# Attention values in column halves, with the output born transposed and the head norm made by a product with ones

## The chip, the cores and the metric

The kernel runs on one core of a Trainium2 chip. The metric is the device time of one execution in microseconds. The engines are named as in the profile: PE (TensorE, with PEld for its weight loads), DVE (VectorE), ACT (ScalarE), POOL (GpSimd) and SP (SyncE, which only issues DMAs here). Each runs its own instructions in order and waits on semaphores; POOL also issues DMAs.

## The reference, cut to what matters

One residual block over 1024 tokens of width 1024: RMS norm, one projection, stick-breaking attention (8 heads of 64) beside gated linear attention (GLA, 4 heads), an output projection, then a routed mixture of 32 experts. The part that the change touches:

```python
for i in range(T // Q_BLOCK):                       # 8 query tiles of 128, keys up to kend
    z = einsum('bqhd,bshd->bhqs', qb, kb) * scale
    a = where(strict, exp(log_sigmoid(z) + tail), 0.0)
    outs.append(einsum('bhqs,bshd->bqhd', a, vb))   # the value product
sb = rms_norm(sb, sb_out_norm_g)                    # per head: mean over its 64 columns
h = h + concat([sb, go], axis=-1) @ w_out
```

All inputs are float32. The output projection and the experts split each operand in a high and a low part and make three products of them (`three`).

## The kernel before, in words

**Stages.** First the projections (to about 249 us). Then attention: 48 steps, one for each query tile i (0 to 7), pair of heads (0 to 3) and up to 512 keys, so a tile of i < 4 has four steps of width 128(i+1), a later one has four of 512 and four of the rest. Then the W_out stage: one output tile after another, eight in all, with the GLA state recurrence, the norm and the routing of the tile before woven in. Last the experts, in blocks of 128 rows.

**An attention step** n, as the engines' loops have it (PE's loop at line 958, ACT's at 1379, DVE's at 1720): PE makes the scores of both heads (`scores`, line 876, each head in its 64 rows of the array), ACT evicts them twice with a sigmoid (1388, 1391), DVE scans them (1731) and multiplies (1736), PE turns the result two steps later (`turn_a`, 893), ACT copies it out (`prob`, 1399), and PE multiplies it with the values three steps later (`values`, 912). There the turned probabilities are the weights (128 keys x 128 queries) and 64 value columns of one head stream through; the output has queries on its partitions and all eight heads side by side in one bank. When a tile is complete, ACT squares it into `o_sq` (1363) and copies it to `o_sb` (1364), and DVE sums the squares by head (1724).

Between scores and transposes and again before the values, PE has `fill` products: 12 units of 8 k steps that make the GLA queries and the output gate. Their place is planned by `fill_plan`, over the first 40 steps, by the width of the steps. Unit f from the fifth on waits until DVE has taken the gate of the unit before it out of bank 7 (`gate_ready`, line 1743).

**The norm and the projection.** The eight-column means of tiles 0 to 6 go through Ln and Exp at once on ACT (1411, 1412), the last tile's after the stage. POOL multiplies tile by tile (`norm_sb`, 618). PE then turns the tile (`turn_sb`, 990), ACT and DVE split it in its high and low part (`sb_high` 1428, `sb_low` 1603), and the W_out products take it as weights.

**Order in the W_out stage.** The orders are written out by hand. PE's loop at 1033 has eight k steps of six products a tile; `read_states`, `turn_h`, `keys_values(t + 2, 0)` (line 934, which waits for `gv_in` from DRAM), `route`, `turn_sb`, `keys_values(t + 2, 1)` and `turn_gla` stand behind named k steps. ACT's loop at 1467, iteration w: `square_h(w-1)`, `go_square(w+1)`, `rstd_h`, `evict_h`, `go_rstd`, `sb_high`, `go_high`, `route_exp(w-1)`. `square_h(t)` writes `v_row[t % 2]` and from t = 2 on waits until the rows of tile t-2 have been scattered (`own_scattered`, line 1440). DVE's loop is at 1876. POOL's loop at 655, for t = 1 to 7: `load_gv(t + 1)`, `load_gate(t)`, `norm_sb(t + 1)`, and from t = 3 on `scatter_own(t - 3)` and `scatter_given(t - 3)`, two indirect DMAs each; ahead of it stand `load_gv(0)`, `load_gv(1)`, `load_gate(0)`, `norm_sb(0)`, `norm_sb(1)`. `norm_sb` waits for one of two counts only:

```python
pool.wait_ge(sb_rstd, 1 if t < TILES - 1 else 2)
```

## Time and profile before

| what | value |
|---|---|
| median of 3 runs | 1219.95 us (1219.72 to 1222.05) |
| profiled execution | 1218.32 us, span 1216.6 us |
| mean granted PE clock | 0.990 |
| busy: PE, DVE, ACT, POOL | 1170.6, 857.5, 732.0, 295.1 us |
| value products (line 912), 576 passes | 69.6 us busy, mean 270 ns |
| weight loads of these | 70.5 us, mean 191 ns |
| scans on DVE (line 1731), 96 | 94.0 us, mean 1020 ns |

All times inside the execution are counted from the start of the span. A float32 product shows as two passes, each a weight load and a matmul. Of passes merged into one row the given time runs from the first start to the last end, and the ends of matmuls are modelled, so a row reaches some 0.2 us into what follows; start-to-start distances are the safer reading. Line numbers of the form L765 are those of the kernel below; L765 to L767 are the three products of `three`, whoever calls it.

### The profile page before, as it was taken

The page shows a single profiled execution, that of the slowest core. Times are in us where ns is not written, and L with a number is a line of the kernel's source. Part 1 is how long each engine was busy: PE and PEld are TensorE (multiplying, and loading weights), DVE is VectorE, ACT ScalarE, POOL GpSimd, SP SyncE. Part 2 cuts the span into 40 slices and gives each one's busy share as a digit, 9 for nine tenths or more (in the row PEclk, how much of TensorE's full clock was granted, in tenths as well). Part 3 has the DMA queues.
Part 4 walks back from the last instruction along what each step waited for, and adds up shares of the span by engine and source line. Part 5 has one row for each costly group of instructions (what it writes and reads, how often), then busy time and mean ns, then how long its engine had stood idle before and what let it go on. Part 6 is the DMA issues. An engine that isn't in the chain of part 4 may idle for free. (4 is left out here: it accounts for less than half of the span.)

```text
span 1216.6 us, 17187 instructions
## 1 busy us (share of the span) xinstructions
PE 1170.6 (96%) x6164; PEld 959.6 (79%) x6164; DVE 857.5 (70%) x975; ACT 732.0 (60%) x894; POOL 295.1 (24%) x250
## 2 busy tenths in 40 slices
PE   5999999999989998999989999999999999999997
PEld 4897777877867776777877878888888888888886
DVE  6721212267656689677677999888988988988894
ACT  5532222366535585232356887887888788788873
POOL 3300000010000002132243236343433433222322
PEclk9999999999989999999989999999999999999999
DMA  8155443010000033356688999999999999999992
GB/s 267 45 188 210 141 162 113 1 53 19 26 18 18 19 122 113 114 190 242 252 298 311 331 385 403 379 400 382 376 384 399 378 380 394 386 367 386 393 377 56
DMA packets 71029, 288.18 MB, mean 237 GB/s; under 512 B 16224, under 2 KB 23409, under 8 KB 46402
## 3 DMA queue, kind: packets, MB, share of 16 engines
q1 hardware_dynamic: 51538, 238.30, 50.8%
q0 software_dynamic: 14064, 30.31, 9.0%
q10 hardware_dynamic: 5376, 18.88, 3.9%
q8 instruction: 33, 0.54, 0.2%
q14 instruction: 18, 0.15, 0.0%
HBM read 248.82 MB, written 54.80 MB: 250 GB/s over the span
## 5 line engine op out<-in xcount | busy, mean ns | idle before, releaser
L1603 DVE TENSOR_TENSOR ew_l<-raw,ew_h 128x2048 fp32r<-128x2048 f32 x192 | 430.7, 2284 | 0.0
L1422 ACT ACTIVATE ew_h<-raw 128x2048 fp32r<-128x2048 f32 x192 | 364.9, 1921 | 53.2 <-PE banks L767 46.4
L765 PE MATMUL banks<-ew_h,xb_h 128*128 128x512 f32 x520 | 205.8, 396 | 1.9 <-issue 1.6
L767 PE MATMUL banks<-ew_h,xb_l 128*128 128x512 f32 x520 | 202.9, 390 | 0.0
L766 PE MATMUL banks<-ew_l,xb_h 128*128 128x512 f32 x520 | 202.5, 389 | 0.0
L1731 DVE TENSOR_TENSOR_SCAN tails<-tails 128x512 f32<-128x512 f32 (+3 forms) x96 | 94.0, 1020 | 62.5 <-ACT tails L1388 62.5
L765 PE MATMUL banks<-win_h,u_h 128*128 128x512 f32 (+1 forms) x320 | 122.6, 383 | 2.8 <-DVE u_l L1603 2.5
L766 PE MATMUL banks<-win_l,u_h 128*128 128x512 f32 (+1 forms) x320 | 118.9, 372 | 0.0
L767 PE MATMUL banks<-win_h,u_l 128*128 128x512 f32 (+1 forms) x320 | 118.8, 371 | 0.0
L765 PEld LDWEIGHTS banks<-ew_h,xb_h 128*128 128x128 f32 x520 | 98.0, 188 | 21.9 <-issue 1.9
L767 PEld LDWEIGHTS banks<-ew_h,xb_l 128*128 128x128 f32 x520 | 97.6, 188 | 20.9
L766 PEld LDWEIGHTS banks<-ew_l,xb_h 128*128 128x128 f32 x520 | 97.7, 188 | 19.2
L765 PE MATMUL banks<-ew_h,a_h 128*128 128x512 f32 x248 | 99.3, 401 | 0.0
L767 PE MATMUL banks<-ew_h,a_l 128*128 128x512 f32 x248 | 97.0, 391 | 0.0
L766 PE MATMUL banks<-ew_l,a_h 128*128 128x512 f32 x248 | 96.8, 390 | 0.0
L702 POOL DMA_INDIRECT out_dram<-y_row,scatter_row x31 | 51.3, 1654 | 158.7 <-ACT y_row L1517 146.5
L601 POOL TENSOR_TENSOR z_l<-z_raw,z_h 128x1024 fp32r<-128x1024 f32 x6 | 14.6, 2437 | 303.2 <-ACT z_h L1308 303.2
L1388 ACT ACTIVATE tails<-banks 128x1024 f32<-128x1024 f32 (+3 forms) x48 | 39.4, 821 | 70.0 <-PE banks L880 58.6
L694 POOL DMA_INDIRECT xb<-rows_dram,gather_idx x28 | 74.4, 2659 | 22.7 <-POOL gather_idx L691 21.6
L912 PEld LDWEIGHTS banks<-v_s,prob 128*128 128x128 f32 x576 | 70.5, 191 | 3.2 <-issue 0.4
L765 PEld LDWEIGHTS banks<-win_h,u_h 128*128 128x128 f32 x320 | 60.5, 189 | 15.6 <-issue 6.1
L912 PE MATMUL banks<-v_s,prob 128*128 128x64 f32 x576 | 69.6, 270 | 0.0
(248 smaller groups left out, 1991.2 us busy)
## 6 DMA issues: line engine op xcount, KB each, us to landing
raw<-in_expert_w_gate SPq DMA_DIRECT2D x64, 1024.0 KB, 8.6
raw<-in_expert_w_down SPq DMA_DIRECT2D x64, 1024.0 KB, 7.2
raw<-in_expert_w_up SPq DMA_DIRECT2D x64, 1024.0 KB, 7.6
rows_dram<-zero_rows ACTq DMA_DIRECT2D x8, 2048.0 KB, 7.6
win_raw<-in_w_in SPq DMA_DIRECT2D x16, 512.0 KB, 5.1
x_in<-in_x SPq DMA_DIRECT2D x8, 512.0 KB, 9.4
raw<-in_w_out SPq DMA_DIRECT2D x4, 1024.0 KB, 4.8
h_row<-in_x SPq DMA_DIRECT2D x8, 512.0 KB, 6.2
```

The costliest lines, as they stand in the source:

```text
L601: nc.gpsimd.tensor_tensor(z_l[b % 2][:, :, :], z_raw[b % 2][:, :, :], z_h[b % 2][:, :, :].bitcast(fp32), SUB).then_inc(z_l_ready, 1)
L694: pool.indirect_dma_start(out=xb[:, :], out_offset=None, in_=rows_dram, in_offset=bass.IndirectOffsetOnAxis(ap=gather_idx[:, :], axis=0), ...
L702: pool.indirect_dma_start(out=out_rows, out_offset=bass.IndirectOffsetOnAxis(ap=row[:, 0:1], axis=0), in_=y[:, :], in_offset=None, bounds_ ...
L765: mm(ps, lh, rh, start=start, stop=False)
L766: mm(ps, lh, rl, start=False, stop=False)
L767: return mm(ps, ll, rh, start=False, stop=stop)
L912: last = mm(o_bank[:, SB_DIM * hd:SB_DIM * (hd + 1)], prob[n % 2][:, h, P * j:P * j + P], v_s[:, u["lo"] // P + j, SB_DIM * hd:SB_DIM * (h ...
L1388: A(tails[u["row"] % 2][:, :, u["col"]:u["col"] + u["w"]], z, ACT.Sigmoid, scale=-1.0).then_inc(c_done, 1)
L1422: A(ew_h[slot % SPLIT][:, :], raw[raw_slot][:, :], ACT.Copy).then_inc(ew_h_ready, 1)
L1603: return V.tensor_tensor(dst, src, high.bitcast(fp32), SUB)
L1731: last = V.tensor_tensor_scan(out=part, data0=part, data1=part, initial=1.0 if u["top"] else row[:, h, c1:c1 + 1], op0=MUL, op1=ALU.min)
```

## The change

In `values` the operands are swapped. The value columns of one head (128 keys x 64) are the weights, the turned probabilities (128 keys x 128 queries) stream through, and head h of the pair writes partitions 64h to 64h+63 of the bank: the output has head dimensions on its partitions and queries along the columns, that is, it is born transposed. The two heads of a pair alternate. `turn_sb` is gone.

The sum of squares by head now runs across partitions: `mean_o` multiplies the squared tile with `head_ones`, two 64x64 blocks of ones, in one product of 512 columns, which gives every element its head's mean. ACT makes the factor of a whole tile by Ln and Exp over 128x512 (`rstd_o`) into `o_rs`, which holds one tile, and POOL multiplies two full tiles. DVE's reductions over `o_sq` are gone. `square_o` reads the copied tile, no longer the bank. `sb_high` and `sb_low` read `o_t` in place of bank 4. Tile 0 gets split buffers of its own, so that it is split while attention still ends.

The order around it: `mean_o(0)` and `mean_o(1)` stand in PE's steps 48 and 50, `mean_o(t + 2)` behind k = 6 of W_out tile t. W_out(0) now begins without waiting for `turn_gla(0)` and `keys_values(1, 0)`, which stand behind its k = 1 and k = 0. On ACT `rstd_o(w + 1)` and `square_o(w + 2)` stand at the head of iteration w, and on DVE `sb_low(0)` ahead of `go_mean(0)`. POOL's loop keeps its order; `norm_sb(t)` waits for the factor of its own tile. `turn_h` waits for `sb_rstd` where it waited for `sb_mixl`. SP loads `gain2` after the first mean and not after the last.

```diff
...
@@ -178,10 +177,14 @@
         gate_out = at("gate_out", R3 + 66 * KB, [P, HALF])
-        o_sb = at("o_sb", R1 + 96 * KB, [P, TILES, HALF])
+        o_t = at("o_t", R1 + 96 * KB, [P, TILES, HALF])
+        o_sq = at("o_sq", R1 + 70 * KB, [P, HALF])
+        mix_first_h = at("mix_first_h", R1 + 72 * KB, [P, PAIRS, P], f32r)
+        mix_first_l = at("mix_first_l", R1 + 74 * KB, [P, PAIRS, P], f32r)
 
...
         wo_l = at("wo_l", R1 + 32 * KB, [P, KT, D], f32r)
+        o_rs = at("o_rs", R1 + 64 * KB, [P, HALF])
         gv_in = [at("gv_in0", R3 + 42 * KB, [P, HALF]), at("gv_in1", R1 + 66 * KB, [P, HALF])]
...
@@ -613,10 +617,8 @@
             def norm_sb(t):
-                pool.wait_ge(sb_rstd, 1 if t < TILES - 1 else 2)
-                rows = o_sb[:, t, :].rearrange("p (h n) -> p h n", n=SB_DIM)
-                nc.gpsimd.tensor_tensor(rows, rows, o_rs[:, t, :].rearrange("p (h a) -> p h a", a=1).broadcast_to(
-                    [P, SB_HEADS, SB_DIM]), MUL).then_inc(sb_normed, 1)
+                pool.wait_ge(sb_rstd, t + 1)
+                nc.gpsimd.tensor_tensor(o_t[:, t, :], o_t[:, t, :], o_rs[:, :], MUL).then_inc(sb_normed, 1)
 
...
@@ -906,13 +908,24 @@
                         pe.wait_ge(kq_out, 2 * TILES)
-                for h in range(2):
-                    hd = 2 * u["pair"] + h
-                    for j in range(u["w"] // P):
-                        last = mm(o_bank[:, SB_DIM * hd:SB_DIM * (hd + 1)], prob[n % 2][:, h, P * j:P * j + P],
-                                  v_s[:, u["lo"] // P + j, SB_DIM * hd:SB_DIM * (hd + 1)], start=first and h == 0 and j == 0,
-                                  stop=True, skip_group_check=True)
+                for j in range(u["w"] // P):
+                    for h in range(2):
+                        hd = 2 * u["pair"] + h
+                        last = mm(o_bank[SB_DIM * h:SB_DIM * (h + 1), P * u["pair"]:P * (u["pair"] + 1)],
+                                  v_s[:, u["lo"] // P + j, SB_DIM * hd:SB_DIM * (hd + 1)], prob[n % 2][:, h, P * j:P * j + P],
+                                  start=first and j == 0, stop=True, skip_group_check=True)
                 last.then_inc(pv_done, 1)
+
+            def mean_o(t):
+                pe.wait_ge(o_squared, t + 1)
+                if t < 2:
+                    pe.wait_ge(beta_done, NZ - 1 + t)
+                else:
+                    pe.wait_ge(sb_rstd, t)
+                    if t >= 3:
+                        pe.wait_ge(vt_ready, t - 2)
+                mm(bank[2 * t if t < 2 else 4], head_ones[:, :], (o_sq if t else o_sq_first)[:, :], start=True,
+                   stop=True).then_inc(o_mean, 1)
 
...
@@ -961,6 +974,10 @@
                 fill(n, 0)
+                if n == NZ:
+                    mean_o(0)
+                if n == NZ + 2:
+                    mean_o(1)
                 if 2 <= n < NZ + 2:
...
@@ -1027,9 +1034,6 @@
 
-            turn_sb(0)
-            turn_gla(0)
-            keys_values(1, 0)
             for t in range(TILES):
...
@@ -1041,28 +1045,31 @@
                         col = slice(HALF * half, HALF * half + HALF)
-                        last = three(bank[2 * (t % 2) + half], mix_h[t % 2][:, k, :], mix_l[t % 2][:, k, :],
+                        mh, ml = (mix_first_h, mix_first_l) if t == 0 and k < 4 else (mix_h[t % 2], mix_l[t % 2])
+                        last = three(bank[2 * (t % 2) + half], mh[:, k, :], ml[:, k, :],
                                      wo_h[:, k, col], wo_l[:, k, col], start=k == 0, stop=k == KT - 1)
...
                         rank_tile(t - 2)
+                    if t == 0 and k in (0, 2):
+                        keys_values(1, k // 2)
                     if t == 0 and k == 1:
-                        keys_values(1, 1)
-                    if k == (0 if t else 2) and t + 1 < TILES:
+                        turn_gla(0)
+                    if k == (0 if t else 4) and t + 1 < TILES:
                         read_states(t + 1)
...
                         turn_h(t - 1)
-                    if k == (2 if t else 3) and t + 2 < TILES:
+                    if k == (2 if t else 5) and t + 2 < TILES:
                         keys_values(t + 2, 0)
...
                         route(t - 1)
-                    if k == 3 and t + 1 < TILES:
-                        turn_sb(t + 1)
-                    if k == 4 and t + 2 < TILES:
+                    if k == (4 if t else 6) and t + 2 < TILES:
                         keys_values(t + 2, 1)
-                    if k == 5 and t + 1 < TILES:
+                    if k == (5 if t else 7) and t + 1 < TILES:
                         turn_gla(t + 1)
+                    if k == 6 and t + 2 < TILES:
+                        mean_o(t + 2)
                     if k == 5 and t == TILES - 1:
...
@@ -1357,11 +1364,22 @@
                 act.wait_ge(pv_done, m + 1)
-                if i:
-                    act.wait_ge(o_mean, i)
                 o_bank = bank[7 if i == TILES - 1 else 6]
-                A(o_sq[:, :], o_bank, ACT.Square, scale=SB_DIM ** -0.5).then_inc(o_squared, 1)
-                A(o_sb[:, i, :], o_bank, ACT.Copy).then_inc(o_out, 1)
+                A(o_t[:, i, :], o_bank, ACT.Copy).then_inc(o_out, 1)
+
+            def square_o(t):
+                act.wait_ge(o_out, t + 1)
+                if t == 1:
+                    act.wait_ge(qk_done, NZ)
+                if t >= 2:
+                    act.wait_ge(o_mean, t)
+                A((o_sq if t else o_sq_first)[:, :], o_t[:, t, :], ACT.Square, scale=SB_DIM ** -0.5).then_inc(o_squared, 1)
+
+            def rstd_o(t):
+                act.wait_ge(o_mean, t + 1)
+                if t:
+                    act.wait_ge(sb_normed, t)
+                rstd_of(o_rs[:, :], bank[2 * t if t < 2 else 4], eps_col[:, :]).then_inc(sb_rstd, 1)
 
...
@@ -1374,6 +1392,15 @@
                 rstd_of(go_rs[:, :], go_ms[:, :], eps_col[:, :]).then_inc(g_rs, 1)
+
+            def sb_high(t):
+                act.wait_ge(sb_normed, t + 1)
+                if t == 1:
+                    act.wait_ge(pv_done, NZ)
+                if t >= 2:
+                    act.wait_ge(wo_done, t - 1)
+                A((mix_h[t % 2][:, 0:4, :] if t else mix_first_h[:, :, :]), o_t[:, t, :].rearrange("p (k n) -> p k n", n=P),
+                  ACT.Copy).then_inc(sb_mixh, 1)
 
...
@@ -1405,12 +1432,14 @@
                     wo_high(WO_SPLIT[n])
+                if n == FILL_SLOTS // 2:
+                    square_o(0)
                 if n == NZ:
                     nc.scalar.preload_act_table_set("natural_log_exp_and_others")
-                    act.wait_ge(o_mean, TILES - 1)
-                    link(A(o_rs[:, 0:TILES - 1, :], o_ms[:, 0:TILES - 1, :], ACT.Ln, bias=eps_col[:, :]))
-                    A(o_rs[:, 0:TILES - 1, :], o_rs[:, 0:TILES - 1, :], ACT.Exp, scale=-0.5).then_inc(sb_rstd, 1)
+                    rstd_o(0)
+                    square_o(1)
                 if n == NZ + 1:
+                    sb_high(0)
                     go_square(0)
...
@@ -1459,13 +1482,14 @@
 
-            sb_high(0)
             evict_o(TILES - 1, NZ - 1)
             go_high(0)
-            act.wait_ge(o_mean, TILES)
-            rstd_of(o_rs[:, TILES - 1, :], o_ms[:, TILES - 1, :], eps_col[:, :]).then_inc(sb_rstd, 1)
             for w in range(TILES):
                 t = w + 1
+                if t < TILES:
+                    rstd_o(t)
+                if w + 2 < TILES:
+                    square_o(w + 2)
                 if w:
...
@@ -1763,7 +1783,8 @@
                 dve.wait_ge(sb_mixh, t + 1)
-                low(mix_l[t % 2][:, 0:4, :], bank[4].rearrange("p (k n) -> p k n", n=P), mix_h[t % 2][:, 0:4, :]).then_inc(sb_mixl, 1)
+                mh, ml = (mix_h[t % 2][:, 0:4, :], mix_l[t % 2][:, 0:4, :]) if t else (mix_first_h[:, :, :], mix_first_l[:, :, :])
+                low(ml, o_t[:, t, :].rearrange("p (k n) -> p k n", n=P), mh).then_inc(sb_mixl, 1)
 
...
@@ -1863,16 +1884,14 @@
             wo_low(2)
+            sb_low(0)
             go_mean(0)
             go_norm(0)
-            sb_low(0)
             next_state(2)
...
             wo_low(3)
-            dve.wait_ge(o_squared, TILES)
-            V.reduce_sum(o_ms[:, TILES - 1, :], heads(o_sq[:, :]), axis=AX.X).then_inc(o_mean, 1)
             for w in range(TILES):
...
```

## Rows read from the trace of the kernel before

**Rows 1.** Busy time by stage: engines' busy us (instructions), PE clock, DMA share, GB/s

```profile
248.70:433.40 184.70, 178.89 (x1129) 140.27 (x1128) 119.98 (x138) 103.06 (x153) 13.85 (x9) 0.98 0.08 25
433.40:476.30 42.90, 40.30 (x315) 32.12 (x314) 40.00 (x41) 36.25 (x42) 4.25 (x6) 1.00 0.43 153
...
534.87:589.00 54.13, 52.71 (x322) 41.26 (x321) 41.00 (x139) 15.41 (x42) 17.98 (x20) 1.00 0.64 238
...
607.00:650.00 43.00, 38.10 (x204) 32.37 (x203) 33.03 (x85) 24.28 (x31) 15.23 (x14) 0.88 0.78 271
...
650.00:1216.00 566.00, 556.93 (x2628) 466.28 (x2628) 489.54 (x323) 441.86 (x372) 202.50 (x145) 1.00 0.96 365
```

**Rows 2.** Timeline of PE around value products: start, us, what, count

```profile
399.99 0.40 PE L767 MATMUL banks<-u_h,z_l 128*128 128x512 f32 x1
400.23 1.89 PE L912 MATMUL banks<-v_s,prob 128*128 128x64 f32 x16
...
406.21 1.00 PE L912 MATMUL banks<-v_s,prob 128*128 128x64 f32 x8
```

**Rows 3.** Timeline of PE: a full-array product, and column-half products of the GLA group

```profile
108.77 0.60 PE L832 MATMUL banks<-log_g,suffix 128*128 128x256 f32 x2
109.20 0.50 PE L834 MATMUL banks<-chunk_sel,log_g 128*128 128x2 f32 x4
...
537.05 1.09 PE L947 MATMUL banks<-state,gq_t 128*64 128x256 f32 x8
...
541.61 0.40 PE L767 MATMUL banks<-wo_h,mix_l 128*128 128x512 f32 x1
541.93 0.66 PE L934 MATMUL banks<-gv_in,k_dec 64*64 64x128 f32 x8
```

**Rows 4.** What fill products waited for (us, times); busy time after the longest wait

```profile
  DVE gate_out L1743: 5.8, 3
...
356.50:360.00 3.50, 3.46 (x9) 2.78 (x10) 1.88 (x3) 0.00 (x0) 0.00 (x0) 0.52 0.22 80
```

**Rows 5.** Timeline at the turn to W_out, in brackets idle before; busy time after it

```profile
472.76 2.48 DVE L1694 SCALAR_TENSOR_TENSOR wo_l<-raw,mix_gain,wo_h 128x1024 fp32r<-128x1024 f32 x2
...
478.63 0.50 PE L765 MATMUL banks<-wo_h,mix_h 128*128 128x512 f32 x1
...
485.04 1.09 PE L947 MATMUL banks<-state,gq_t 128*64 128x256 f32 x8 [1.23 <-DVE state L1711]
...
492.52 0.70 PE L934 MATMUL banks<-gv_in,k_dec 64*64 64x128 f32 x8 [2.21 <-DVE state L1711]
...
493.10:496.50 3.40, 3.40 (x13) 2.67 (x11) 1.47 (x5) 0.00 (x0) 0.00 (x0) 0.51 0.02 5
```

**Rows 6.** Timeline of POOL, ACT and DVE during one W_out tile (w=3)

```profile
534.09 1.05 POOL L618 TENSOR_TENSOR o_sb<-o_sb,o_rs 128x512 f32<-128x512 f32 x1
541.02 1.04 POOL L642 DMA_INDIRECT rows_dram<-v_row,dest  x1 [5.88 <-DVE dest L1857]
...
545.96 0.59 POOL L607 DMA_DIRECT2D gv_in<-gv_dram  x1
...
536.16 0.20 ACT L1460 ACTIVATE stat<-stat 128x1 f32<-128x1 f32 x1 [2.21 <-DVE stat L1821]
539.35 1.06 ACT L1441 ACTIVATE v_row<-h_row 128x1024 f32<-128x1024 f32 x1 [2.98 <-DVE h_row L1785]
...
542.20 1.06 ACT L1452 ACTIVATE v_t<-banks 128x512 f32<-128x512 f32 x2
...
540.08 0.15 DVE L1857 SCALAR_TENSOR_TENSOR dest<-rank,expert_of 128x2 int32<-128x2 f32 x1
```

**Rows 7.** Timeline of PE in that tile: the transposes that leave

```profile
545.72 0.63 PE L990 MATMUL banks<-ident,o_sb 128*128 128x128 f32 x4
```

**Rows 8.** Landing of gv loads, from issue; the wait for a landed scatter

```profile
DMA to landing us min/median/max: 3.0/3.5/6.6
...
POOL xb L667 <- DMA rows_dram<-v_row,dest: 6.3, 1, 6.3
```

More of the change, by code:

```diff
@@ L110, in hybrid_block_kernel @@
         kq_rs = const("kq_rs", [P, 2, SB_HEADS])
-        o_ms = const("o_ms", [P, TILES, SB_HEADS])
-        o_rs = const("o_rs", [P, TILES, SB_HEADS])
+        head_ones = const("head_ones", [P, P])
         glr_s = const("glr_s", [P, 2, RANK])
@@ L453, in _ @@
                 sp_e.dma_start(h_row[n][:, :], x_t[n]).then_inc(hx[n], 16)
-            sp_e.wait_ge(o_mean, TILES)
+            sp_e.wait_ge(o_mean, 1)
             sp_e.dma_start(gain2[:, :], ffn_norm_g.partition_broadcast(P)).then_inc(gain2_in, 16)
@@ L547, in link @@
                 pool.wait_ge(psmall, chain[0])
-            for tile, value in ((ident, 0.0), (causal_neg, 0.0), (suffix, 0.0), (chunk_sel, 0.0), (before, 1.0),
+            for tile, value in ((ident, 0.0), (causal_neg, 0.0), (suffix, 0.0), (chunk_sel, 0.0), (head_ones, 0.0), (before, 1.0),
                                 (ones_b, 1.0), (eps_col, EPS)):
@@ L555, in _ @@
                 nc.gpsimd.memset(suffix[r, r], 1.0 / TAU)
+                nc.gpsimd.memset(head_ones[r, r], 1.0)
                 last = nc.gpsimd.memset(chunk_sel[r, b:b + 1], 1.0 / TAU)
@@ L981, in turn_gla @@
                 last.then_inc(g_turned, 1)
-            def turn_sb(t):
-                pe.wait_ge(sb_normed, t + 1)
-                if t:
-                    pe.wait_ge(sb_mixl, t)
-                if t >= 2:
-                    pe.wait_ge(vt_ready, t - 1)
-                for p in range(PAIRS):
-                    last = nc.tensor.transpose(bank[4][:, P * p:P * p + P], o_sb[:, t, P * p:P * p + P], ident[:, :])
-                last.then_inc(sb_turned, 1)
             def turn_h(t):
                 pe.wait_ge(h_ready, t + 1)
-                pe.wait_ge(sb_mixl, min(t + 2, TILES))
+                pe.wait_ge(sb_rstd, min(t + 3, TILES))
                 pe.wait_ge(g_mixed, min(t + 2, TILES))
@@ L1422, in high @@
                 A(ew_h[slot % SPLIT][:, :], raw[raw_slot][:, :], ACT.Copy).then_inc(ew_h_ready, 1)
-            def sb_high(t):
-                act.wait_ge(sb_turned, t + 1)
-                if t >= 2:
-                    act.wait_ge(wo_done, t - 1)
-                A(mix_h[t % 2][:, 0:4, :], bank[4].rearrange("p (k n) -> p k n", n=P), ACT.Copy).then_inc(sb_mixh, 1)
             def go_high(t):
@@ L1436, in square_h @@
                 if t == 1:
-                    act.wait_ge(sb_turned, 2)
+                    act.wait_ge(sb_mixl, 2)
                 if t >= 2:
@@ L1720, in _ @@
             for n in range(NZ + 4):
-                if n - 4 in TILE_END and n - 4 < NZ - 1:
-                    i = TILE_END[n - 4]
-                    dve.wait_ge(o_squared, i + 1)
-                    V.reduce_sum(o_ms[:, i, :], heads(o_sq[:, :]), axis=AX.X).then_inc(o_mean, 1)
                 if n < NZ:
```

6 lines of the change are left out of this document (3 added, 3 removed).

## The prediction

> **What bounds the kernel now.** I read the stages first. From 248.7 to 433.4 us (attention, while the fill products still run) PE is busy for 178.89 of 184.70 us and DVE for 119.98: PE paces it. From 433.4 to 476.3 (last query tile, no fill left) DVE is busy for 40.00 of 42.90 us, PE 40.30, ACT 36.25: the scans and their wait for ACT share the pace. The W_out stage, three tiles of it from 534.87 on, has PE at 52.71 of 54.13 us, so PE paces that too, 18.0 us a tile, but the chain of norm, routing and gate beside it is nearly as long. The 566 us of experts that follow are PE at full clock; whatever the earlier stages gain or lose is handed on whole [rows 1]. The profiled execution took 1218.3 us (span 1216.6), 1.6 below the median 1219.95, so sums carry over as they are.
>
> **The products themselves.** An old value product of a 512-wide step issues 16 passes and takes 1.89 us, a 256-wide one 8 passes in 1.00: 0.445 us for each 128 keys of a head pair [rows 2]. The new form issues as many passes, each with 64 weight columns and 128 moving ones, the two heads in different column halves. The trace has this shape in the state products of the GLA group: 8 passes of 128 columns in 0.65 us, though a 256-column pass on the full array starts 0.22 us before the next (two in 0.43), that is 0.11 for 128 columns: 8 in a row would be 0.88 plus their latency. Two must run at once. The state reads say it for 128 rows: 8 passes of 256 columns in 1.09 us, against 8 x 0.22 = 1.7 one after another [rows 3]. So 0.65 us for 256 keys and, 4 more passes being 2 x 0.11, 0.87 for 384, 1.09 for 512, 0.43 for 128; old, by 0.445 for each 128 keys up or down from the two rows, 1.00, 1.45, 1.89 and 0.56. Entering halves costs: from the last fill pass to a column-half product 0.32 us, to an old value product 0.24 [rows 2, 3]; 0.09 is lost per step. Leaving is the same, as the old one also had to switch, to the scores' row halves. Net per step 0.71, 0.49, 0.26 and 0.04 us for widths 512, 384, 256, 128. Up to the end of the fill there are 16, 8, 8 and 8 such steps: 11.4 + 3.9 + 2.1 + 0.3 = 17.7 us. (Upper end, if the first pair's longer gap falls under the switch: 20.)
> The Trainium skill (TensorE: Matmul & The Clock Gate, Part 3, The mechanism) says that a weight load overlaps a running matmul only where the row group differs; both heads here use all 128 rows, so by it the load of every pair would stand bare. By it, with the page's load time (64 columns over 1.2, 53 ns, an estimate from that page), each pair would cost 0.05 us more and the 17.7 us that come next would be 6. The trace disagrees: the state reads are such halves with all 128 rows, and 4 pairs x 0.22 us of streaming plus the 0.2 tail already fill their 1.09 us [rows 3].
>
> **What of it reaches the end.** The fill must wait for DVE's gate product after each fill unit: three waits, 5.8 us in all, today [rows 4]. The gate hangs on the scan of the same step, not on PE, so what the value product between saves there is lost: about 1.4 us over seven units. After the longest of them PE ran 3.5 us at clock 0.52, the lower of its two levels (1.2 GHz) [rows 4]; if one more wait grows long enough for that it costs up to 1.7 us. In the last tile's 8 steps PE would save 5.7 us, but DVE and ACT are as full as PE: only the removed reduction and Square (0.7 us) count. Attention: -17.0 us.
> The turn to W_out: now PE waits for states (1.23 and 2.21 us) and then runs 3.4 us at clock 0.51 [rows 5]. After the change sb_low(0) comes ahead of go_mean on DVE, behind wo_low(2), which ends at 475.2; so W_out(0) can start at 476.0 and not at 478.6 [rows 5], and the states are made under its first products. Against this stand the mean product before values(47) (two passes of 512 columns, 0.86 us by twice the 256-column row [rows 3]) and the Ln and Exp over 128x512 on ACT (1.2 us by the 1.06 of two 128x512 copies plus their link [rows 6]), before prob(47). I take -5 us (-2.6 if all waits are only moved, -6.5 if all vanish). Each later tile: turn_sb leaves (four transposes, 0.63 us with a tail of 0.2 that the next products cover [rows 7]), mean_o comes with 0.86 and a switch: +0.5, six times, 3 us; norms on POOL stay 1.05.
>
> **The queue that is easy to miss.** o_rs now holds one tile, and rstd_o(w+1) is made at the head of ACT's iteration w, behind route_exp(w-2). Before, norm_sb(t+1) in POOL's loop found its factor ready: at 534.09, ahead of W_out(3), it normed tile 5 [rows 6]. Now POOL stands there until iteration w = t begins. Queued behind it, in order, are scatter_own(t-3), scatter_given(t-3), load_gv(t+2), load_gate(t+1). Take w=3. route_exp ends at 536.36, Ln and Exp end at 537.6, the norm at 538.75. Four scatters follow; today they take from their release by dest (540.23) to the gv load at 545.96: 5.7 us [rows 6]. The gv load is issued at 544.5 and lands 3.5 us later by the median of such loads (3.0 to 6.6) [rows 8]: 548.0. PE wants this tile at 541.93 [rows 3]: a wait of 6.1 us (5.6 to 9.2) where there is none, since today the load runs a tile ahead. In parallel square_h(2), which overwrites v_row, waits for scatter_own(0), issued by 541.9 and landed at 545 to 547.7 (3.0 after issue by the quickest such load; 6.3 is the one wait for this scatter that shows [rows 8]), instead of 539.35; its chain up to the copied transposes takes 3.9 us (539.35 to 543.26 today [rows 6]) and so ends at 548.9 to 551.6, where PE then stands before the logits. Less 0.4 for turn_sb, 5.7 to 7.2 us per tile for w = 3, 4 and 5. PE's idle of that length was followed by half clock in both places that rows 4 and 5 show; 3.4 us of it cost 1.7. I take 8 us x 3 = 24. In w=6 there is no gv load, but square_h(5) and so route(5) wait the same way: 7.5 us. For w = 0 to 2 no scatter is in the way and the gv load is late by 0.3 to 1.6 us: 2.5 in all. w=7 has no norm. Sum of this stage: +34 us, bounds 20 (no half clock, w=6 absorbed, waits at their low ends) and 42.
>
> **Sum.** -17.0 - 5 + 3 + 34 = +15; the slack before the experts, where PE is busy 38.10 of 43.00 us [rows 1], may take back 3 to 4 of it. Forecast +11.5 us: 1231.5. Ends: -20 - 6.5 + 3 + 20 = -3.5, and -14 - 2.6 + 3 + 42 = +28.
>
> **Rivals.**
> A. The POOL wait costs little: POOL's loop finds the factor early enough, or loads and scatters still come ahead of need. For: POOL is busy 17.98 of 54.13 us [rows 1], and its queue stands 5.88 us at a time for nothing [rows 6]. Against: order, not load, is what holds it. Then -17 - 5 + 3 + 3 = -16, 1204 us: faster. It decides if the gv row lands by the third k of each W_out tile.
> B. Column halves don't run together in this accumulating form, or their loads stand bare. Then 128 keys cost 4 x 0.109 = 0.44 us as before, the switches 40 x 0.09 = 3.6 us come on top, and attention goes from -17 to +4: 1252 us, or about 1241 if only half is lost. For: the only such rows are short bursts of 8. Against: those rows [rows 3].
> C. The stall is there but partly hidden (scatter issue shorter without DVE beside it, landing at 3 us, no half clock): +20 for the stage, time 1215 to 1224, about no change.
>
> **How the numbers follow.** Forecast (stall whole, 1224 to 1242) 0.62; A 0.15; C 0.13; B 0.10. The likeliest one's own range is 1224 to 1242. The range for 8 in 10 takes in C and part of A and of B: 1207 to 1243. Measured differences under 0.2% (2.4 us) can't be told from none. Slower by more: the forecast and B, 0.72. Same: half of C, 0.07. Faster: A and the other half of C, whose low end has the longest attention gain, 0.21.
>
> **What would show it.** Value products of a 512-wide step in about 1.1 us and 16 passes; stage up to the end of fill about 168 us long instead of 184.7; gate waits in all 7 to 8 us; W_out(0) starting 2.6 us earlier after the last value product. In W_out: state products (L934) waiting for DMA gv_in by 6 us in three tiles; POOL's norm at the head of each tile and scatters behind it; square_h waiting for rows_dram; tiles 3 to 6 of 24 to 26 us; clock near 0.9 there. Wrong would be: a value step above 1.5 us (B), W_out tiles of 18 to 19 us throughout (A), or a last attention tile that becomes shorter by over 3 us, which would mean DVE did not pace it.

## The result and the profile after

| | before | changed |
|---|---|---|
| median | 1219.84 us (1217.78 to 1222.05, 10 runs) | 1226.33 us (1223.26 to 1235.67, 10 runs) |
| ratio | | 1.0066, interval 1.0044 to 1.0088 |
| profiled execution | 1218.32 us, span 1216.6 | 1223.26 us, span 1221.5 |
| mean granted clock | 0.990 | 0.986 |

Slower by 6.5 us. The forecast was 1231.5 with 1224 to 1242 as its own range. The kernel before was timed again beside each group of experiments, with medians of 1220.1 to 1221.3 us, and the ratios given below are to those; times of different groups can differ by some 1.5 us for that alone. The two profiled executions lie 4.9 us apart; their balance is drawn up below, and it leaves out what the median has beyond it. The ten executions of the changed kernel spread over 12.4 us, those of before over 4.3, and the slowest (1235.67) has a mean clock of 0.972, the fastest 0.986: the slower an execution, the lower its clock.

The page of the changed kernel: PE is busy for 12.6 us less than before (1170.6), in a span that is 4.9 us longer.

```profile
span 1221.5 us, 17171 instructions
...
PE 1158.0 (95%) x6148; PEld 923.7 (76%) x6148; DVE 849.9 (70%) x967; ACT 741.2 (61%) x906; POOL 290.5 (24%) x253
```

Its timeline of PE around value steps (start, us, what, passes) answers to [rows 2, 3]: 1.09 us for 512 keys and 0.88 for 384, where the old form took 1.89 and some 1.45. The first value pass starts 0.32 us after the last fill pass.

```profile
403.19 0.40 PE L769 MATMUL banks<-u_h,z_l 128*128 128x512 f32 x1
403.51 0.88 PE L914 MATMUL banks<-prob,v_s 128*64 128x128 f32 x12
...
408.25 1.09 PE L914 MATMUL banks<-prob,v_s 128*64 128x128 f32 x16
```

Its stages answer to [rows 1] (columns as there; then one row for each of the W_out tiles 2 to 6). The last fill product starts at 417.14 us where it stood at 431.32. In the W_out tiles look at PE's busy time against the length: tile 2 is full, in each of tiles 3 to 6 PE is idle for 3.2 to 5.3 us, and in tiles 3 to 5 its busy time has itself grown, from 17.89 to between 19.53 and 19.93 us, for the same products: that is the clock of 0.86 to 0.93.

```profile
248.70:417.90 169.20, 163.10 (x1122) 110.44 (x1122) 116.27 (x130) 101.27 (x148) 12.55 (x6) 0.98 0.09 27
417.90:460.50 42.60, 35.35 (x328) 22.52 (x323) 40.84 (x43) 37.35 (x42) 4.29 (x7) 1.00 0.45 161
...
496.87:514.76 17.89, 17.89 (x104) 13.66 (x103) 13.42 (x45) 6.79 (x18) 2.56 (x3) 1.00 0.48 158
514.76:540.02 25.26, 19.93 (x105) 15.16 (x104) 13.40 (x45) 6.75 (x18) 6.71 (x7) 0.86 0.55 175
540.02:563.94 23.92, 19.53 (x106) 14.87 (x105) 13.43 (x45) 6.79 (x18) 6.67 (x7) 0.93 0.54 195
563.94:587.52 23.58, 19.64 (x108) 15.01 (x107) 13.42 (x45) 6.67 (x17) 6.67 (x7) 0.93 0.49 178
587.52:609.69 22.17, 18.96 (x90) 15.28 (x89) 8.89 (x33) 5.64 (x16) 11.09 (x10) 0.85 0.62 227
```

What PE waited for from 456 us to 640 (us in total, times, longest): the load that was in time before (in tile 3 the product that takes it follows at once [rows 3]) now is late, in tiles 3, 4 and 5 (5.3, 4.4 and 3.9 us, and 0.8 in tile 1); in tile 6, which has no such load, the router waits for ACT.

```profile
PE banks L947 <- DMA gv_in<-gv_dram: 14.4, 4, 5.3
PE banks L1017 <- ACT v_t L1475: 3.2, 1, 3.2
```

And why, in POOL's timeline of tile 3 (idle before in brackets). It answers to [rows 6]: there the norm ran at 534.09, ahead of W_out(3); here POOL stands 15.3 us for ACT's factor, and the four scatters, which had been free to go, and the load of the GLA rows come behind it. ACT's two rows below show the second arm of the stall: the row buffer `v_row` is free again only when the scatter has landed, and `route` waits for `v_t`, which ACT copies behind that write in its own queue.

```profile
515.36 1.28 POOL L621 TENSOR_TENSOR o_t<-o_t,o_rs 128x512 f32<-128x512 f32 x1 [15.32 <-ACT o_rs L1208]
516.82 1.08 POOL L644 DMA_INDIRECT rows_dram<-v_row,dest  x1 [0.17 <-DVE given L1860]
518.20 1.01 POOL L644 DMA_INDIRECT rows_dram<-v_row,dest  x1 [0.30 <-issue]
519.51 0.98 POOL L652 DMA_INDIRECT table_dram<-given,dest  x1 [0.30 <-issue]
520.80 0.98 POOL L652 DMA_INDIRECT table_dram<-given,dest  x1 [0.30 <-issue]
521.78 0.60 POOL L611 DMA_DIRECT2D gv_in<-gv_dram  x1
```

```profile
515.18 0.61 ACT L1376 ACTIVATE o_sq<-o_t 128x512 f32<-128x512 f32 x1
525.01 1.06 ACT L1464 ACTIVATE v_row<-h_row 128x1024 f32<-128x1024 f32 x1 [9.21 <-DMA rows_dram<-v_row,dest]
```

Two windows show what the wait leaves behind: PE idle for 5.3 us, and then 3.4 us of full work at clock 0.50. The record of the clock has it at this level for 6.8 us, from 524.1 to 530.9, so it fell while PE stood, and 4.3 us of it lie on work.

```profile
521.30:526.60 5.30, 0.01 (x2) 0.01 (x2) 0.00 (x0) 1.59 (x3) 1.86 (x3) 0.76 0.61 102
526.60:530.00 3.40, 3.40 (x14) 2.59 (x15) 1.38 (x4) 2.32 (x8) 0.00 (x0) 0.50 0.01 2
```

Starts in the two profiled executions, us, read from the trace:

| start of | before | changed | difference |
|---|---|---|---|
| last fill product | 431.32 | 417.14 | -14.2 |
| last value pass | 475.62 | 460.28 | -15.3 |
| W_out(1) | 499.36 | 478.10 | -21.3 |
| W_out(3) | 534.87 | 514.76 | -20.1 |
| W_out(7) | 604.99 | 609.69 | +4.7 |
| first expert product | 636.51 | 640.37 | +3.9 |
| end of the span | 1216.6 | 1221.5 | +4.9 |

Tiles 3 to 6 took 18.07, 18.09, 18.09 and 15.86 us before, and 25.26, 23.92, 23.57 and 22.17 after: +24.8 us, against the 20.1 won ahead of them.

### The profile page after: what moved, and what is told of

The parts are those of the page before. It is cut to its first block and busy times, and to the rows that moved or that the text cites. A ratio compares the mean times of both kernels' runs of the same rounds, so it can differ in the third digit from the quotient of the medians.

```text
span 1221.5 us, 17171 instructions
## 1 busy us (share of the span) xinstructions
PE 1158.0 (95%) x6148; PEld 923.7 (76%) x6148; DVE 849.9 (70%) x967; ACT 741.2 (61%) x906; POOL 290.5 (24%) x253
## 5 line engine op out<-in xcount | busy, mean ns | idle before, releaser
L605 POOL TENSOR_TENSOR z_l<-z_raw,z_h 128x1024 fp32r<-128x1024 f32 x6 | 14.6, 2440 | 294.4 <-ACT z_h L1315 294.4
L769 PEld LDWEIGHTS banks<-win_h,u_l 128*128 128x128 f32 x320 | 60.4, 189 | 10.6
L768 PEld LDWEIGHTS banks<-win_l,u_h 128*128 128x128 f32 x320 | 60.6, 189 | 9.2
```

Of the source, the lines that this page charges most:

```text
L605: nc.gpsimd.tensor_tensor(z_l[b % 2][:, :, :], z_raw[b % 2][:, :, :], z_h[b % 2][:, :, :].bitcast(fp32), SUB).then_inc(z_l_ready, 1)
L768: mm(ps, lh, rl, start=False, stop=False)
L769: return mm(ps, ll, rh, start=False, stop=stop)
```

## Experiments on the stall

### The norm in its turn

The changed kernel with one edit in POOL's loop: tile t is normed in iteration t and not one iteration ahead. Its factor is made in ACT's iteration t-1, so it is there when POOL comes.

```diff
-            norm_sb(1)
...
-                if t + 1 < TILES:
-                    norm_sb(t + 1)
+                norm_sb(t)
```

> The changed kernel with one thing moved in POOL's loop: norm_sb(t) stands in loop step t in place of norm_sb(t+1), so POOL waits for the factor of tile t only after load_gv(t+1), load_gate(t) and the scatters of the step before have been issued. Theory 1 (the whole loss is POOL's in-order queue standing at norm_sb): W_out tiles 3 to 6, now 25.3, 23.9, 23.6, 22.2 us, go back to 18.1, 18.1, 18.1, 15.9 plus about 0.5 each for the mean product, no PE wait for gv_in, no ACT wait for rows_dram; time 1226.3 - 23 = 1203 (1198 to 1208), ratio to before 0.982 to 0.990. Theory 2 (the Ln and Exp over whole tiles on ACT and the mean products stretch the chain of each W_out tile, POOL only shows it): tiles stay above 21 us, time above 1215.

Measured: 1198.18 us (5 runs), ratio 0.9818 (0.9804 to 0.9832). The W_out tiles from 1 on take 17.95, 17.89, 17.93, 17.93, 17.99 and 15.52 (tile 6, 15.86 before); the waits for the GLA rows and for the scattered rows are gone. POOL's timeline of this kernel: the norm now waits 2.29 us for its factor, and the scatters wait for their own data (`dest`), not for the norm; the load is issued at 505.47 and used at 519.86.

```profile
496.14 1.28 POOL L621 TENSOR_TENSOR o_t<-o_t,o_rs 128x512 f32<-128x512 f32 x1 [2.29 <-ACT o_rs L1206]
500.53 1.08 POOL L643 DMA_INDIRECT rows_dram<-v_row,dest  x1 [3.10 <-DVE dest L1876]
...
505.47 0.61 POOL L611 DMA_DIRECT2D gv_in<-gv_dram  x1
```

So the whole loss of the change, and some 21 us that it had won, hung on one position in one queue. The second theory is out, since the Ln and Exp over whole tiles and the mean products are all still there. This version is faster than both kernels.

### The same wait put into the kernel before

The kernel before with a wait of the same kind ahead of the norm, for a signal that ACT gives at about the time at which the changed kernel's factor comes.

```diff
                 if t + 1 < TILES:
+                    if t >= 2:
+                        pool.wait_ge(r_ratio, t - 1)
                     norm_sb(t + 1)
```

> The kernel before with one wait added: in POOL's loop norm_sb(t+1) waits, from t=2 on, for r_ratio >= t-1, which ACT signals at the end of route_exp(t-2), the point behind which the changed kernel makes the factor. Nothing else is changed. Theory 1: PE waits for gv_in in W_out tiles 3 to 5 and for the routing chain in tile 6, as in the changed kernel, about 1.3 us less per tile since no Ln and Exp stand between; tiles 3 to 6 longer by 4 to 6 us each, time 1219.8 + 19 = 1239 (1234 to 1246). Theory 2: POOL's waiting has cover, time 1220 to 1225.

Measured: 1249.81 us (4 runs), ratio 1.0236 (1.0211 to 1.0261). The mechanism is confirmed, for the new attention and the ones product are not in this kernel: PE waits for the GLA rows in tiles 3, 4 and 5. The size is a miss, some 10 us above what I had expected. Tiles 3 to 6 take 29.51, 23.12, 28.09 and 22.07 us, although the waits (below) are no longer than in the changed kernel (4.9, 4.1 and 4.3 us for the load).

```profile
PE banks L936 <- DMA gv_in<-gv_dram: 13.2, 3, 4.9
PE banks L1012 <- ACT v_t L1454: 2.7, 1, 2.7
```

The windows of tile 3 of this kernel show where it went: after the wait PE runs 15.7 us at clock 0.51. Counted over tiles 3 to 6 the low clock holds for 41 us here (17.1, 3.4, 13.7 and 6.8 us, tile by tile) and for 20.5 us in the changed kernel (6.8, 3.4, 3.4 and 6.8).

```profile
541.10:545.90 4.80, 0.00 (x0) 0.00 (x0) 0.75 (x2) 3.37 (x9) 1.65 (x3) 0.84 0.63 111
545.90:561.60 15.70, 15.63 (x60) 12.63 (x61) 5.97 (x14) 0.62 (x2) 0.00 (x0) 0.51 0.46 168
```

### Which arm of the stall holds PE

The changed kernel, once with the GLA load issued one tile earlier, ahead of the norm, and the scatters left behind it; once with the scatters put ahead of the norm, which puts the load of the next iteration right behind it.

```diff
# load ahead
+            load_gv(2)
...
-                if t + 1 < TILES:
-                    load_gv(t + 1)
                 load_gate(t)
+                if t + 2 < TILES:
+                    load_gv(t + 2)
                 if t + 1 < TILES:
                     norm_sb(t + 1)
```

```diff
# scatters ahead
-                if t + 1 < TILES:
-                    norm_sb(t + 1)
                 if t >= 3:
                     scatter_own(t - 3)
                     scatter_given(t - 3)
+                if t + 1 < TILES:
+                    norm_sb(t + 1)
```

> The changed kernel with only the GLA value loads taken out of the queue: load_gv(t+2) is issued ahead of norm_sb(t+1), the scatters stay behind it. It tells the two waits apart. Theory 1a (two parallel chains of nearly equal length, gv load to keys_values and scatter landing to square_h to route): the wait for gv_in disappears, PE waits instead for v_t before route in tiles 3 to 6 by 4 to 6 us, tiles get only 1 to 1.5 us shorter, time 1226.3 - 5 = 1221 (1218 to 1224). Theory 1b (the gv load alone carries it): tiles 3 to 5 fall to 18.6 us, time about 1208.

> The changed kernel with the scatters of loop step t issued ahead of norm_sb(t+1), load_gv(t+1) still behind norm_sb(t). Theory 1a: the gv load then follows the norm directly, is issued about 2 us after the start of a W_out tile and lands 3.5 us later, about when keys_values wants it: at most 1 us of wait per tile, square_h not held, time 1203 to 1208. Theory 1b (the gv load alone carries it): same. Theory 2: above 1215.

Measured: load ahead 1222.87 us (10 runs), ratio 1.0029 (1.001 to 1.0049), tiles 3 to 6 of 26.83, 25.09, 20.33 and 21.85; scatters ahead 1198.84 us (4 runs), ratio 0.9821 (0.9805 to 0.9836), better than expected. With the load ahead the wait is not gone but stands at the router, in four tiles (5.3, 2.2, 2.1 and 3.2 us). That is 4.1 us less of waiting in these tiles than in the changed kernel (16.9), but the low clock holds for 27.3 us of these tiles and not for 20.5, so that little is left of it:

```profile
PE banks L1018 <- ACT v_t L1476: 12.8, 4, 5.3
```

The two arms lie side by side, and taking away one leaves the other: what a wait that vanishes from the list has saved is not known until the next one in the tile is looked at. With the scatters ahead the norm still waits 8 to 14 us for its factor, and that costs nothing, since nothing that is late stands behind it:

```profile
497.42 1.28 POOL L621 TENSOR_TENSOR o_t<-o_t,o_rs 128x512 f32<-128x512 f32 x1 [13.68 <-ACT o_rs L1208]
498.65 0.56 POOL L611 DMA_DIRECT2D gv_in<-gv_dram  x1
...
501.81 1.06 POOL L644 DMA_INDIRECT rows_dram<-v_row,dest  x1 [1.84 <-issue]
```

### How much of the stall is the clock

16 products of 512 columns whose results nobody reads, ahead of the waiting state product in tiles 3, 4 and 5, in the changed kernel and in the kernel before with the wait. They fill the wait with work.

```diff
+                    if k == 2 and t in (3, 4, 5):
+                        for _ in range(16):
+                            mm(bank[2 * ((t + 1) % 2)], mix_h[t % 2][:, 0, :], wo_h[:, 0, 0:HALF], start=True, stop=True)
```

> The changed kernel with 16 extra products of 512 columns (about 3.6 us of PE) ahead of keys_values(t+2, 0) in W_out tiles 3, 4 and 5, into a bank that nothing reads; they lie in the time in which PE waits for gv_in (5.3, 4.4 and 3.9 us). Theory 1 (what the trace shows as half clock behind each wait is caused by PE's idle time and costs about 2 us a tile on top of the wait): no stretch at clock 0.5 behind the waits, these three tiles 1.5 to 2.5 us shorter each, time 1226.3 - 6 = 1220 (1217 to 1223). Theory 2 (the half clock costs nothing, since the tile is paced by DVE, ACT and the transfers then): 1225 to 1228.

> The kernel of e2_stall_in_before (the old kernel with POOL's wait added) with the same 16 extra products in W_out tiles 3 to 5. Its tiles 3 and 5 ran 14 and about 10 us at half clock behind waits of 4.9 and 4.3 us. Theory 1: that is why it came out 10 us above what was expected; without the idle time it falls by 9 to 14 us, to 1236 to 1241, near the 1239 expected for e2. Theory 2 (the waits themselves were mis-sized): 1247 to 1251.

Measured, in the changed kernel: 1226.04 us (7 runs), ratio 1.0053 (1.0033 to 1.0073), the median not moved; inconclusive. In its profiled execution, its slowest, tiles 4 and 5 are 22.33 and 21.89 us (1.6 and 1.7 shorter), while tile 3 is 29.35 with 13.7 us of low clock behind a wait that is down to 1.4 us, and tile 6, which has no filler, is 24.71 us (22.17 without filler in the others), since its wait for `v_t` is 5.2 us and not 3.2. In the kernel with the wait: 1243.07 us (4 runs), ratio 1.0189 (1.0153 to 1.0226), 6.7 us less than without the filler, where 9 to 14 had been expected. In the profiled executions tiles 3 to 5 are 14.3 us shorter, and tile 6 pays 2.0 us of it back (24.07 against 22.07). The low clock is gone from tiles 3 to 5; two of them:

```profile
536.10:559.00 22.90, 21.43 (x123) 16.68 (x122) 13.12 (x45) 5.10 (x14) 6.87 (x7) 1.00 0.54 176
559.00:581.30 22.30, 21.48 (x124) 16.66 (x124) 13.09 (x45) 5.13 (x14) 6.86 (x7) 1.00 0.54 190
```

So a stalled tile at full clock takes 22.9, 22.3 and 21.1 us, 3.0 to 4.8 more than the 18.1 of before. The changed kernel's tile rows, without any filler, say about the same: PE is idle 5.3, 4.4, 3.9 and 3.2 us in tiles 3 to 6, 16.8 in all, and busy 2.0, 1.6, 1.7 and 3.4 us longer than in the same tiles of the kernel with the norm in turn (17.93, and 15.52 for tile 6), 8.7 in all. By this account, which rests on the traces since the filler in the changed kernel did not move the median, a third of the stall's price there is the low clock. The filler is no cure: it doesn't keep the clock up every time.

## Experiments on the products and the turn

### One head after the other

The kernel with the norm in turn, and the loop over heads outside the loop over key blocks, so that the column halves no longer alternate.

```diff
-                for j in range(u["w"] // P):
-                    for h in range(2):
-                        hd = 2 * u["pair"] + h
+                for h in range(2):
+                    hd = 2 * u["pair"] + h
+                    for j in range(u["w"] // P):
```

> The kernel of e1_norm_in_turn with the two loops of the value product exchanged: all key tiles of head 0, then all of head 1, so that the two column halves no longer alternate in program order. Theory A (PE's queue starts a product of the free column half ahead of a waiting one, as the state reads L947 suggest, whose order is also one half after the other): the halves still run in pairs for the most part, a 512-wide step takes 1.1 to 1.3 us, time 1198 to 1202. Theory B (the alternation is what makes them run together): the passes go one behind another at 0.11 us, a 512-wide step takes 1.9 us, attention loses its gain of some 16 us, time 1213 to 1218.

Measured: 1207.66 us (4 runs), ratio 0.9886 (0.9858 to 0.9914), 9.5 us above the alternating order by the medians, 8.3 by the ratios. The answer lies between the two expectations: a 512-wide step takes 1.58 us, a 384-wide 1.15, a 256-wide 0.66, no more than alternating. In the 512-wide step the first pass of the second head, ninth in the order, starts with the fifth of the first (390.03 us, where the first started at 389.54). So the second head starts four passes ahead of its turn: of the eight passes of each head four run beside the other head's and four by themselves, 12 slots of 0.11 us and not 8 or 16. In the 256-wide step, with four passes a head, all run in pairs.

```profile
384.09 0.66 PE L912 MATMUL banks<-prob,v_s 128*64 128x128 f32 x8
...
389.54 1.58 PE L912 MATMUL banks<-prob,v_s 128*64 128x128 f32 x16
```

### The turn in its old order

The kernel with the norm in turn, with a part of the new order taken back: `turn_gla(0)` and `keys_values(1, 0)` ahead of W_out(0), and `sb_low(0)` behind `go_norm(0)`. The places of `read_states(1)`, `keys_values(2, c)` and `turn_gla(1)` in W_out(0) stay as in the change.

```diff
+            turn_gla(0)
+            keys_values(1, 0)
             for t in range(TILES):
...
-                    if t == 0 and k in (0, 2):
-                        keys_values(1, k // 2)
                     if t == 0 and k == 1:
-                        turn_gla(0)
+                        keys_values(1, 1)
...
-            sb_low(0)
             go_mean(0)
             go_norm(0)
+            sb_low(0)
```

> The kernel of e1_norm_in_turn with the old order at the turn from attention to W_out: turn_gla(0) and keys_values(1, 0) ahead of W_out(0), keys_values(1, 1) behind its k = 1, and on DVE sb_low(0) behind go_norm(0). Theory 1 (the new order is worth what W_out(0) starts earlier and what its waits on the states cost): W_out(0) starts 2 to 3 us after the last value product and not 0.9, waits of 1 to 2 us for the states come back; +3 to +6 us, time 1201 to 1204. Rival (only the missing transposes and the early split bring the gain, the order nothing): 1198 to 1199.

Measured: 1200.71 us (4 runs), ratio 0.984 (0.9819 to 0.9861); the intervals of the two overlap, and the time lies between the two forecasts, 1.7 us above the rival's and 0.3 below the other. The trace decides. From the last value pass to the start of W_out(1) it is 18.9 us, against 18.7 with the new order and 23.7 before. W_out(0) starts 2.6 us after the last value pass instead of 0.95, but is 16.3 us long instead of 17.7, since less is woven in. So the rival's account of the turn was right: these places are worth 0.2 us of its gain. The profiled execution is late by 3.4 us already at the last value pass, ahead of anything that the edit touches, with more of the low clock (30.0 us in all, against 17.7).

### The last tile's mean earlier, in the kernel before

If not the order, what? In the kernel before ACT stood 6.5 us at the turn for the last tile's sums of squares, and the squares of GLA tile 1 stood behind it. Here DVE makes these sums right after `sb_low(0)`.

```diff
             sb_low(0)
+            dve.wait_ge(o_squared, TILES)
+            V.reduce_sum(o_ms[:, TILES - 1, :], heads(o_sq[:, :]), axis=AX.X).then_inc(o_mean, 1)
             next_state(2)
...
             wo_low(3)
-            dve.wait_ge(o_squared, TILES)
-            V.reduce_sum(o_ms[:, TILES - 1, :], heads(o_sq[:, :]), axis=AX.X).then_inc(o_mean, 1)
```

> The kernel before with one reduction moved on DVE: the sum of squares of the last query tile, which stood behind wo_low(3), now stands behind sb_low(0). ACT waits 6.5 us for it before go_square(1). Theory 1 (that wait, not the transposes or the place of keys_values, made W_out(0) long: go_square(1) late, state late, 2.2 us of PE wait and then half clock): go_square(1) starts 2 us earlier, the 2.2 us wait and the half clock behind it go, W_out(0) falls from 20.7 to 17 to 18 us, time 1219.8 - 3 = 1217. Rival (the wait is set by the states of the GLA group themselves): W_out(0) stays above 20 us, time 1219 to 1221.

Measured: 1217.66 us (11 runs), ratio 0.997 (0.9956 to 0.9984), 3.6 us below the kernel before timed beside it (1221.28). ACT's wait for `o_ms` is gone, the state products wait 0.47 us where they waited 2.21 [rows 5], the low clock that followed is gone too (window below: 1.00, was 0.51), and W_out(1) starts at 495.99 us, 3.4 us earlier. From the last value pass to W_out(1) it is 20.4 us instead of 23.7. So in the old kernel 3.3 us, more than half of the turn's 5.9, come from taking this one wait away. The changed kernel has no such wait either; that its gain comes by the same way is argued from this, not shown.

```profile
490.70 0.65 PE L934 MATMUL banks<-gv_in,k_dec 64*64 64x128 f32 x8 [0.47 <-DVE state L1711]
```

```profile
493.00:496.50 3.50, 3.50 (x19) 2.90 (x18) 2.39 (x2) 0.63 (x1) 2.08 (x3) 1.00 0.10 34
```

### The fill spread wider

With the cheaper value step PE is idle in the last attention tile (35.35 of 42.60 us busy). The kernel with the norm in turn, with the fill planned over 42 and over 44 steps instead of 40.

```diff
-FILL_SLOTS = 40
+FILL_SLOTS = 42
```

> The kernel of e1_norm_in_turn with the fill products spread over 42 steps and not 40 (FILL_SLOTS = 42), so two steps of the last query tile carry fill; the splitting of the W_out weights moves two steps later with it. Theory 1 (the last tile is paced by DVE and ACT and has 5.9 us of idle PE in its 42.0): about 4 us of fill go into idle time, 1198 - 3 = 1195. Rival (the last tile's end hangs on the splits of the W_out weights on ACT and DVE, which now come later and run into the start of W_out): 0 to +4 us, 1198 to 1202.

> As e7_fill_42, with 44 steps. Theory 1: the idle time of the last tile is used up at about 8 us of fill moved, -4 to -5 us, 1193 to 1194. Rival as there, and larger since two of the four splits of the W_out weights now lie behind the last step: +2 to +8 us, 1200 to 1206.

Measured: 42 steps 1196.97 us (4 runs), ratio 0.9811 (0.9793 to 0.983), the lowest median of all, but not to be told from the 1198.18 of 40 steps, and between the two forecasts (in the traces W_out(0) starts 1.0 us earlier, at 458.9); 44 steps 1202.23 us (4 runs), ratio 0.9853 (0.9835 to 0.9871), slower. With 44 the last fill product starts at 429.6 us, nearly as late as in the kernel before (431.3), and a wait for the gate and one for the state stand in the last tile and at the turn; the rows behind them run at the low clock (1.98 us, where the value step takes 1.09). W_out(0) starts at 465.7 us, with 40 steps at 459.9.

```profile
432.44 1.98 PE L912 MATMUL banks<-prob,v_s 128*64 128x128 f32 x16 [2.42 <-DVE gate_out L1761]
...
459.83 1.98 PE L958 MATMUL banks<-state,gq_t 128*64 128x256 f32 x8 [3.24 <-DVE state L1733]
```

## Why the prediction was right, point by point

The mechanism was right: the products in column halves save time, and the norm in POOL's queue costs more than they save. The number owes something to luck. The profiled execution, 1223.26 us, lies below the range of 1224 to 1242; the median lies in it since most executions had more of the low clock. And the +11.5 was made of terms that were too high by 12 us in all and others that were too low by 5.

**The products.** Right to 0.01 us for each width (1.09, 0.88, 0.66 against 1.09, 0.87, 0.65), and the entry of 0.32 us also. Rival B is out. Both heads use all 128 rows, and 16 passes of 128 columns fit into 1.09 us where 0.11 each one after another would be 1.76. By the rule that I took from the Trainium skill (TensorE: Matmul & The Clock Gate, Part 3, The mechanism), that a weight load overlaps a running matmul only where the row group differs, the loads would stand bare and a 512-wide step would be 0.4 us longer than it is, an estimate with that page's load time. Here the trace disagrees with the rule; the same section also lets a load go ahead into the background weight buffer, and by that way the loads need not have stood bare. No run here shows which it is.

**Up to the end of the fill: -17.7 was too much.** The failing step is a count. I took 16, 8, 8 and 8 steps, those that carry fill; but the values of a step come three steps later, and ahead of the last fill product there stand only 14, 6, 8 and 8. With these my own steps give 0.71 x 14 + 0.49 x 6 + 0.26 x 8 + 0.04 x 8 = 15.3 us. The trace, start to start over these 36 steps, has 18.2 us saved inside and 3.6 paid at the entries: 14.6. The gate waits grew from 5.8 to 6.1 us, not by 1.4. The last fill product came 14.2 us earlier where 16.3 were forecast.

**The last tile.** From the last fill product to the last value pass 1.2 us were saved (forecast 0.7), with PE's work down by some 5 us: DVE is busy for 40.84 of 42.60. Right.

**The turn.** -5.9 us from the last value pass to W_out(1), forecast -5. The size was right and the reason mostly not: I gave it to the new order, of which the tested part is worth 0.2, while taking away the wait for the last tile's sums brings 3.3 us in the old kernel. The other 2.4 us were not taken apart; 0.8 of them hang on the norm running one tile ahead (-5.1 with the norm in turn). That W_out(0) would start 2.6 us earlier after the last value pass was right (3.0 to 0.2). With the norm in turn the new order starts it 1.7 us earlier than the old one, and W_out(0) is 1.4 us longer for it.

**The product with ones.** Forecast +0.5 per tile, +3 in all. Where nothing stalls, tiles 2 to 5 take 17.89 to 17.99 us, against 18.1 before: no cost in the balance. But the price was right. In tile 3 of the changed kernel the second W_out product behind the two passes starts 1.32 us after the last one ahead of them; without the passes it would be two product spacings, 0.46 us. So they cost 0.86 us, as forecast, and about 0.4 leaves with the transposes.

```profile
537.55 0.39 PE L769 MATMUL banks<-wo_h,mix_l 128*128 128x512 f32 x1
537.78 1.02 PE L927 MATMUL banks<-o_sq,head_ones 128*128 128x512 f32 x2
538.24 0.79 PE L767 MATMUL banks<-wo_h,mix_h 128*128 128x512 f32 x1
538.87 0.39 PE L768 MATMUL banks<-wo_l,mix_h 128*128 128x512 f32 x1
```

What the sum lacked is a wait that goes: before, each such tile stood some 0.5 us for `chosen_any` (2.0 us in four tiles), and with the norm in turn none does. Why it goes was not traced.

**The stall.** Mechanism, place and both arms right: the norm stands for its factor, four scatters and the load are behind it, PE waits in three tiles for the load and in tile 6 for the router, and square_h for the landed rows. The term that was mis-sized is this one: 24.8 us in tiles 3 to 6 against 31.5 forecast for them. In tile 3 two terms miss in opposite directions. The load was issued 7.0 us after the tile's start, not 9.6, mostly since ACT had the factor ready at 515.3, 0.5 us into the tile, where I had put it 2.7 us in: ACT's `route_exp` ahead of it had ended at 514.0, before the tile began, and I had taken it to end 1.5 us into the tile, as before. It landed 4.8 us later, not 3.5 (before, the load that went out first behind four scatters, at 527.88, had taken 4.8 too, and was the nearer row than the median of all), and PE wanted it 0.6 us earlier in the tile. From the 6.1 us of the forecast these give 6.1 - 2.6 + 1.3 + 0.6 = 5.4, and 5.33 was measured. Tiles 4 and 5 waited 4.4 and 3.9 us. The low clock was forecast at about 1.7 a tile, and PE's busy time in tiles 3 to 5 grew by 2.0, 1.6 and 1.7. For tile 6 I took 7.5, it was 6.3. For tiles 0 to 2 I took 2.5; one wait of 0.8 us for the load shows, in tile 1.

**The tail.** 0.8 us taken back between the start of W_out(7) and the experts (3.5 forecast). The span then ends 1.0 us later still; that was not traced to a cause, and from the first expert product to the end the thirteen traced kernels, whose experts are the same, differ by 2.1 us (579.7 to 581.8).

**The sum.** -14.2 - 1.2 - 5.9 + 1.1 (tiles 1 and 2) + 24.8 - 0.8 + 1.0 = +4.8 us for the profiled pair. The forecast's +11.5 was too high by 6.7 us in the stall, by 4.4 in tiles 0 to 2 and the product with ones and by 0.9 at the turn, and too low by 1.6 in the attention, 2.7 in the tail and 1.0 at the end. The median lies 6.5 us up and not 4.9, since the profiled execution was the fastest of the ten; the others have a lower clock.

**Rival A** (1204 us) is near the number of a kernel without the stall: with the norm in turn it is 1198. Its sum had 3 us for late loads and 3 for the product with ones, and neither came.

## What to carry to other kernels

When an operation's input becomes "just made" instead of "made long ago", walk the in-order queue behind it, DMA issues above all: here one elementwise operation that waited held back a load and four scatters that had nothing to do with it, and cost some 28 us (1226.33 against 1198.18). Move such an operation to the place in its queue where its input is ready, or put what is urgent ahead of it; and don't stop at the first wait removed, since a second one of the same length may lie beside it. And count the instances of a cheaper operation where they execute, not where they are planned.

## What the runs showed of the hardware that was not expected

- Where PE had stood for 4 to 5 us the granted clock went to the lower of its two levels, for a time that differs from place to place and from kernel to kernel: 3.4 us behind the changed kernel's waits of 4.4 and 3.9, 6.8 us from within its wait of 5.3, 17.1 us from within the wait of 4.9 of the kernel before with the wait, and 13.7 us behind a wait of only 1.4 that the filler had left. Such a wait cost between 1.6 and 6.6 us beyond itself. Kernels with such waits spread: 1223 to 1236 us, against 1197 to 1201 with the norm in turn.
- Products in different column halves need not alternate strictly to run together: blocks of four passes did so in full (0.66 us for eight), blocks of eight for half of their passes (1.58 us against 1.09), since the second block started four passes ahead of its turn and no earlier (with blocks of six, too, the seventh pass starts with the third).
- The two row scatters of tile 3 landed 5.1 us after their issue by the median, and the load of the GLA rows behind them after 4.8, against a median of 3.5 for such loads before [rows 8]. The same load, first behind four scatters, had taken 4.8 us before too and took 4.6 with the norm in turn. With the scatters ahead of the norm, where such a load goes out right behind the norm, the loads of the W_out stage took 2.9 to 3.1.
- POOL's product of two full tiles took 1.28 us, 0.23 more than the one with the broadcast factor [rows 6].
